# A two-layer hybrid decoder step: w_in columns as filler, an earlier out-norm, an LRU without a reciprocal, part of the SSD on GpSimd

## What is computed

```
h = adaLN1(rms(x));  x += 0.5 * gate1 * (silu(h @ Wg) * (h @ Wu)) @ Wo
u = adaLN2(rms(x)) @ w_in               # [SSD | RG-LRU | HGRN2 | MLA]
y_a = ssd(u_a) * silu(z)                # chunked scan with a state
y_b = lru(u_b) * gelu(gate)
      # r = sigmoid(..), a = exp(-8 r softplus(-lam))
      # bterm = sqrt(-expm1(2 log a)) * (i * xb),  h = a h + bterm
y_c = hgrn2(q, fz, iv) * silu(g)
y_d = attention(prompt), and over 8 cached pages per sample sequence
y   = rms over each 64 features of concat(y_a .. y_d), times out_norm
x  += gate2 * (y @ w_out)
h = adaLN3(rms(x));  x += 0.5 * gate3 * SwiGLU2(h)
```

## Time and profile before

| | |
|---|---|
| Median of 3 runs | 1909.21 us (1907.89 to 1918.09) |
| The profiled execution | 1913.51 us; its span 1911.8 us |
| PE busy / weight loads | 1771.8 us (93%) / 1524.4 us (80%) |
| DVE, ACT, POOL busy | 957.6, 610.9, 237.4 us |
| Mean granted TensorE clock | 0.944 of full speed |
| Chain that ended last | PE 80%, DVE 14%, ACT 3%, DMA 1% |
| Layer 0: w_in's products, mixing, w_out | begin at 311, 466 and 695 us |
| Layer 1: the same | begin at 1249, 1390 and 1614 us |

### The profile page before, as it was taken

How to read it: one execution, slowest core, us unless ns; L and a number is a source line. 1 busy time by engine, 2 the same in 40 slices (tenths; PEclk the granted TensorE clock), 3 DMA queues, 4 the chain that set the end, 5 groups by cost and what they waited for, 6 DMA issues and landing times.

```text
span 1911.8 us, 28829 instructions
## 1 busy us (share of the span) xinstructions
PE 1771.8 (93%) x11864; PEld 1524.4 (80%) x11864; DVE 957.6 (50%) x1729; ACT 610.9 (32%) x972; POOL 237.4 (12%) x434
## 2 busy tenths in 40 slices
PE   4999999999989788999989999999998887899998
PEld 3999996667667556999979999967766664699998
DVE  3544432465775644354445444236767745444443
ACT  2433321033231324343334333111433233333331
POOL 8000003510044000000000000072003210000000
PEclk8999999999887889999999999999998788999999
DMA  9566647862011253554453544493201123435542
GB/s 316 192 198 202 207 144 227 272 213 84 1 53 42 101 186 116 166 182 131 162 172 130 178 135 159 149 255 106 93 25 35 38 67 132 132 133 176 169 145 67
DMA packets 206275, 272.06 MB, mean 142 GB/s; under 512 B 11778, under 2 KB 182238, under 8 KB 206144
## 3 DMA queue, kind: packets, MB, share of 16 engines
q1 hardware_dynamic: 188240, 236.90, 37.9%
q0 software_dynamic: 17904, 33.33, 6.1%
HBM read 264.68 MB, written 5.50 MB: 141 GB/s over the span
## 4 chain that ended last, share of the span: by engine, by line
PE 80%; DVE 14%; ACT 3%; DMA 1%; issue 1%; SPq 0%; DVEq 0%; ACTq 0%
PE bank L782 16%; PE bank L784 16%; PE bank L783 16%; PE bank L913 10%; PE bank L1048 4%; PE bank L1309 4%; PE bank L719 2%; DVE sq L2269 2%; PE bank L1221 1%; PE bank L709 1%; DMA ring<-in_w_ada_dram 1%; DVE big L1995 1%; PE bank L1021 1%; PE bank L1191 1%; DVE zs L1628 1%
## 5 line engine op out<-in xcount | busy, mean ns | idle before, releaser
L784 PE MATMUL bank<-hT_r,ring_r 128*128 128x320 f32 x1408 | 440.5, 313 | 0.0
L784 PEld LDWEIGHTS bank<-hT_r,ring_r 128*128 128x128 f32 x1408 | 267.5, 190 | 0.0
L1636 DVE TENSOR_TENSOR ring_r<-ring,lat_pages_r 128x2048 fp32r<-128x2048 f32 (+1 forms) x68 | 151.4, 2229 | 162.4 <-ACT lat_pages_r L1335 162.4
L782 PE MATMUL bank<-hT_r,lat_pages_r 128*128 128x320 f32 x704 | 218.9, 311 | 13.5 <-DVE gates_r L1668 13.5
L783 PE MATMUL bank<-gates_r,lat_pages_r 128*128 128x320 f32 x704 | 219.3, 312 | 0.0
L784 PE MATMUL bank<-big_r,ring_r 128*128 128x320 f32 x704 | 218.0, 310 | 0.0
L913 PE MATMUL bank<-hT,ring 128*128 128x320 f32 x736 | 209.6, 443 | 4.7 <-DVE hT L1662 4.7
L913 PEld LDWEIGHTS bank<-hT,ring 128*128 128x128 f32 x736 | 140.9, 194 | 65.2 <-issue 11.6
L1335 ACT ACTIVATE lat_pages_r<-ring 128x2048 fp32r<-128x2048 f32 (+1 forms) x68 | 126.4, 1862 | 142.8 <-DMA ring<-in_w_ffn_in_dram 69.4
L782 PEld LDWEIGHTS bank<-hT_r,lat_pages_r 128*128 128x128 f32 x704 | 134.0, 190 | 19.0 <-issue 18.5
L783 PEld LDWEIGHTS bank<-gates_r,lat_pages_r 128*128 128x128 f32 x704 | 133.9, 190 | 0.0
(11 more groups left out here) (536 smaller groups left out, 3252.8 us busy)
## 6 DMA issues: line engine op xcount, KB each, us to landing
ring<-in_w_ffn_in_dram SPq DMA_DIRECT2D x88, 1024.0 KB, 6.1
ring<-in_w_ada_dram SPq DMA_DIRECT2D x60, 1024.0 KB, 6.0
ring<-in_w_ffn_out_dram SPq DMA_DIRECT2D x32, 1024.0 KB, 5.2
ring<-in_w_in_dram SPq DMA_DIRECT2D x22, 1024.0 KB, 7.3
sqk<-in_w_ada_dram POOLq DMA_DIRECT2D x24, 512.0 KB, 7.6
ring<-in_w_ffn_out_dram SPq DMA_DIRECT2D x16, 768.0 KB, 4.4
lat_pages<-in_cache_mla_latent_dram POOLq DMA_DIRECT2D x128, 64.0 KB, 2.2
ring<-in_w_out_dram SPq DMA_DIRECT2D x8, 1024.0 KB, 9.2
```

The costliest lines, as they stand in the source:

```text
L782: mm(out, w_h, x_h, start=start, stop=False)
L784: return mm(out, w_l, x_h, start=False, stop=stop)
L1636: go(v.tensor_tensor(slot_r(n, nk, 256), slot(n, nk, 256), w_hi_r[g % HI][:, 0:nk].bitcast(F32), ALU.subtract), w_low)
```

## The change

- **Filler.** The chunks are reordered: `fz` before `gate` before `q`, `iv`, `g`. The last six chunks (`FILL0 = 19`: `q`, `iv`, `g`, 48 products) are no longer computed by `win`. `fill(n)` issues the next n of their products, all into bank 7, at places in the mixing; `score(b, 4)` puts one behind each of pages 1 to 4 of sequences 0, 1 and 2. `keep_busy` is gone.
- **Order ahead of the SSD.** The transposes of the convolution's last columns, softplus, and the SSD's sums of dt come before the attention's probabilities are turned; DVE computes the SSD's decay before it takes the prompt attention's output, which PE now writes to bank 4.
- **Outputs.** Since `hT` is still read, the mixers' outputs go to a ring slot held for that purpose (`hold`, `mixer_out`): chunks 0, 1 and 4 to 7. Only the LRU's go to `hT`, and only after the last chunk. The list puts an entry without a load at that slot each time its turn comes, until `w_out` is done; the other loads have four slots.
- **Out-norm.** Order of batches: SSD, LRU, attention of the prompt, HGRN2, attention of the samples. ACT takes the root of the sum, with scale and epsilon in the same instruction, in halves; DVE inverts and multiplies in `scale`. PE's products are single, in bank 7. Batches 0 to 2 lie before and between HGRN2's products with the states (L1221).
- **LRU.** (1 + a^2) * tanh(s) in place of 2 lt/(1+lt): ACT adds a square, DVE does one instruction.
- **GpSimd** runs `spread_b` and the states' decay, behind `store_latents` and before the loads of pages for sequences 4 and 5.

```diff
-       (1284, 256), (1540, 256), (1796, 256), (2052, 256), (2308, 256)]
+       (1796, 256), (1284, 256), (1540, 256), (2052, 256), (2308, 256)]
+FILL0 = 19
+HOLD_AT = (11, 11)
-BATCH = [(0, 0, T), (2, 0, T), (4, 0, T), (6, 0, TP), (6, TP, T)]
+BATCH = [(0, 0, T), (2, 0, T), (6, 0, TP), (4, 0, T), (6, TP, T)]
...
+        def skip_held():
+            if held[0] == len(tl) % RING:
+                tl.append((None, 0, 0, *held[1]))
...
+        def mixer_out(l):
+            slot_now = carve(ring, (pos["mixed", l] % RING) * SLOT, 3, 2, T)
+            return [slot_now[:, 0], hT[:, 2:4], slot_now[:, 1], slot_now[:, 2]]
...
+                    pool.wait_ge(ssd_dve, at(ssd_dve, 3))
+                    spread_b(0)
+                    pool.wait_ge(ssd_act, at(ssd_act, 3))
+                    pool.wait_ge(ssd_pe, at(ssd_pe, 4))
+                    for j in range(2):
+                        ends = Es[:, j, P:].rearrange("p (b t) -> p b t", b=NB)[:, :, TS - 1]
+                        pool.tensor_tensor(ssd_state[:, j], ssd_state[:, j], ends.unsqueeze(2).to_broadcast([P, NB, P]),
+                                           ALU.mult).then_inc(decayed, 1)
+                    pool.wait_ge(ssd_pe, at(ssd_pe, 5))
+                    spread_b(1)
                     pool.wait_ge(group_used, at(group_used, 1))
                     load_pages(2)
...
-                        for _ in range(n):
-                            mm(bank[7][:, 0:64], c("ident"), c("ones")[:, 0:64], start=True, stop=True)
+                    def fill(n):
+                        for i, k in itertools.islice(fills, n):
+                            _, _, t, c0 = WCH[i]
+                            if k == 0:
+                                tile_ready(pe, pos["win", l, t])
+                                if i == FILL0:
+                                    pe.wait_ge(att_q, at(att_q, 1))
+                                else:
+                                    pe.wait_ge(*taken(i - 1))
+                            w = slot(pos["win", l, t], 8, WIN[t][1])
+                            ins = mm(bank[7][:, 0:T], w[:, k, c0:c0 + P], hT[:, k], start=k == 0, stop=k == KD - 1)
...
+                    def out_norm(n, half):
+                        if half == 0:
+                            pe.wait_ge(on_sq, at(on_sq, n + 1))
+                        if n or half:
+                            pe.wait_ge(on_root, at(on_root, 2 * n + half))
+                        _, c0, c1 = BATCH[n]
+                        mm(bank[7][:, c0:c1], c("ones64"), norm_tmp(n)[:, half], start=True, stop=True).then_inc(on_pe, 1)
...
-                        o.go(f(lt[:, j], lr[:, j], ACT.Tanh, scale=nlam8[:, j:j + 1]), lru_act)
+                        o.go(f(lt[:, j], lr[:, j], ACT.Tanh, scale=nlam8[:, j:j + 1]))
+                    o.go(f(lm, la, ACT.Square), lru_act)
                     ac.wait_ge(lru_dve, at(lru_dve, 1))
-                    o.go(f(lm, lm, ACT.Sqrt, scale=2.0), lru_act)
+                    o.go(f(lm, lm, ACT.Sqrt), lru_act)
...
-                    do(v.tensor_scalar(lm, lt, 1.0, None, ADD))
-                    do(v.reciprocal(lm, lm))
-                    do(v.tensor_tensor(lm, lm, lt, MUL), lru_dve)
+                    do(v.scalar_tensor_tensor(lm, lm, 1.0, lt, ADD, MUL), lru_dve)
...
+                        ve.wait_ge(on_root, at(on_root, 2 * n + 2))
+                        do(v.reciprocal(x, x))
```

More of the change, by code:

```diff
@@ L984, in _ @@
                     ins.then_inc(mla_pe, 1)
-                    win(20)
+                    pe.wait_ge(conv_done, at(conv_done, 1))
+                    for i in range(FILL0 - 3, FILL0):
+                        pe.wait_ge(*taken(i))
+                    for k in range(KD):
+                        ins = pe.transpose(bank[k // 4][0:27, (k % 4) * P:(k % 4 + 1) * P], last_cols[:, k], c("ident"))
+                    ins.then_inc(turned, 1)
                     pe.wait_ge(mla_dve, at(mla_dve, 7))
@@ L1139, in _ @@
                     new_states(0).then_inc(ssd_pe, 1)
-                    score(1)
+                    fill(4)
+                    turn(1)
+                    fill(4)
+                    score(1, 4)
                     pe.wait_ge(ssd_dve, at(ssd_dve, 6))
@@ L1522, in att_root, with on_square, on_sqrt @@
                         o.go(f(rk[:, b % 2], rk[:, b % 2], ACT.Sqrt), att_rk)
+                    def on_square(n):
+                        ac.wait_ge(mixed, at(mixed, n + 1))
+                        k0, c0, c1 = BATCH[n]
+                        if n == 2:
+                            ac.wait_ge(on_scaled, at(on_scaled, 1))
+                        o.go(f(norm_tmp(n), mixer[k0 // 2][:, :, c0:c1], ACT.Square), on_sq)
+                    def on_sqrt(n):
+                        _, c0, c1 = BATCH[n]
+                        for half in range(2):
+                            ac.wait_ge(on_pe, at(on_pe, 2 * n + half + 1))
+                            o.go(f(norm_tmp(n)[:, half], bank[7][:, c0:c1], ACT.Sqrt, bias=eps, scale=1.0 / 64), on_root)
                     def soft_exp(g):
@@ L2228, in add_from_states @@
                                            bank[bk][:, at_col:at_col + 2 * L].rearrange("p (j n) -> p j n", j=2), ADD))
+                    ve.wait_ge(win_done, at(win_done, len(WCH)))
+                    go(v.tensor_tensor(mixer[1], lh, gelu, MUL))
+                    for n in range(3):
+                        o.tell(mixed)
                     spread_v(0)
                     spread_v(1)
+                    o.settle()
                     go(v.memset(hs[:, :, 0], 0.0))
@@ L2255, in _ @@
                     o.settle()
-                    do(v.tensor_tensor(hT[:, 4:6], oacc, gh, MUL))
-                    for n in range(4):
-                        o.tell(mixed)
+                    do(v.tensor_tensor(mixer[2], oacc, gh, MUL))
+                    o.tell(mixed)
+                    scale(2)
                     att_inv(5)
```

302 lines of the change are left out of this document (147 added, 155 removed), and 4 rows, old and new, of the table WCH.

## The result

| | before | after |
|---|---|---|
| Median of 7 runs | 1913.14 us | 1927.28 us (1924.0 to 1939.09) |
| Ratio, with 95% interval | 1 | 1.0089 (1.0065 to 1.0113) |
| The profiled execution; its span | 1913.51; 1911.8 us | 1924.00; 1922.3 us |
| PE, DVE, ACT, POOL busy | 1771.8, 957.6, 610.9, 237.4 us | 1729.5, 940.0, 620.7, 252.1 us |
| Mean granted clock, profiled | 0.944 | 0.928 |

A forecast was written before the change was run, and what follows sets the result against it. The prediction took PE to bound the FFN and a chain of hand-overs the mixing. A to D gave −38.9 us, E +4 and F +9, together −25.9, so a median of 1883 us, range 1861 to 1902.

The forecast's parts named there:

- A: First chunk to the SSD's transposes: 36.07 us becomes about 25.2, paced by DVE, as chunks move away; −10.9 us a layer.
- B: SSD's transposes to HGRN2: shorter LRU formula, less 0.8 us of page fills left on the path; −3.2 us a layer.
- C: HGRN2's products with the states: out-norm sums and the LRU's product with gelu now stand ahead; +3.0 us a layer.
- D: End of the mixing: ACT's out-norm root no longer waits for DVE's inversion; −8.7 us, layer 1 some 0.7 less.
- The LRU's -4.0: Part of B: the LRU's tanh-to-root steps become an ACT square and one DVE instruction; −4.0 us with its hand-over.
- F: Clock: constants around sequences 4 and 5 go unreplaced; +4.5 us a layer, +9 in all, ends −5 and +20.
- E: Weight ring with one slot held: FFN tile 1 and two layer 0 tail tiles land late; +4 us in all.
- Rival 2: Fills lie on the path in the mixing: a third of their 26 us shows, +17.6, giving 1901 us; chance 0.15.
- rival 4: Clock falls through the whole mixing, 0.83 to 0.60 giving 1926 us; slower from about 0.64 down; chance 0.05.
- Rival 3: GpSimd is dear (5.3 us and more) or slows DVE: +3 to 6 us a layer, 1892 us; chance 0.10.

The follow-up runs named there:

- z_all: Changed kernel with x_tail's order, x_busy's constants, y_sp's early softplus and z_order's order around the SSD's new states; 1898.1 us, 0.9940 to before.
- z_order: x_tail with the order of the kernel before around the SSD's new states, on both DVE and PE; 1916.3 us, 1.0030 to before.
- x_empty: Changed kernel with only one 64-column constant per filler chunk, the last six chunks not computed; 1915.7 us, 1.0029 to before.
- x_tail: Changed kernel with the out-norm's prompt-attention and HGRN2 batches moved out of the third softmax's way; 1912.9 us, 1.0007 to before.
- z_all2: z_all run once more, unchanged; 1897.6 us on one chip, 0.9935 to before.
- x_const: Changed kernel with its 48 filler products per layer replaced by 64-column constants, the last six chunks not computed; 1916.9 us, 1.0017 to before.
- y_pool: x_tail with GpSimd's two spreads and two decays back on DVE; 1926.6 us, 1.0088 to before.
- z_none: Kernel before without any of its 152 constants in a layer; 1923.4 us, 1.0071 to before.
- x_busy: Changed kernel with constants put back in the second half of the mixing; 1920.1 us, 1.0035 to before.
- v_more: z_all with 42 more constants in a layer, in the second half; 1907.2 us, 0.9980 to before.
- y_sp: x_tail with softplus and the instructions that feed it moved earlier, into DVE's wait for chunks; 1910.3 us, 0.9993 to before.

## Why the prediction was wrong

Against the forecast, the four sections are short by 39 us in the profiled executions: A by 11, B by 18, C by 3, D by 8. The transposes stood at 469.8 us where 465 was forecast, w_out at 699.6 where 675 was.

- **A, right in size but not reached.** The step failed at "with PE thinned out DVE paces" and its 25.2 us, which came to 28.7 in layer 0: softplus and the copies of the last columns, which chunks had covered, were counted as DVE's work and not as PE's wait of 5.01 us, with half the clock behind it. That the sixth chunk's time would just cover the wait for the rotary queries was 0.9 and 2.4 us too good. z_all has A at -10.0 and -9.3.
- **B, wrong, and the largest miss of a section.** "Most of that hides ... I leave 0.8 on the path": layer 0 and 1 lost 7.6 and 10.3 us against the forecast. The clock is not the reason, with 0.90 and 0.86 where 0.86 and 0.88 had been; PE's idle time grew by 6.2 and 4.7 us. The forecast had no term for the new order around the SSD's states, in which PE waits for DVE's scores and turned states. z_all, with the old order there, has B at 75.8 and 75.7 at a clock of 0.90, so a part is that order; z_order had next to nothing of it by itself. The LRU's -4.0 is right (-5.8 and -3.4 alone). How much is the filler's isn't taken apart: x_empty, with next to no filler, still has B at 77.0 and 77.5, but at a clock of 0.77 and 0.78. And 12 of the 48 fills stand in A, where the forecast counted them; what it set against 39.3 us of constants as 26 us of products was 19 us.
- **C, +3.0, with F's +4.3 behind it: right in the sum** (8.7 and 8.6 against 7.3), and that is partly luck. The records of L1298 took 2.7 us more, not 4.3, and the four sums before their end some 4.4 us, not 2.2, most of them at half clock too.
- **D, -8.7: the mechanism was right, its cover wrong.** "ACT is never behind DVE" came true for the out-norm's root. What was missed is who then waits for ACT: the softmax's exponential, 5.6 us. x_tail has -8.5 and -7.7.
- **E, +4: the sum is near, its parts are not.** The two waits for ada tiles in layer 0 take 3.4 us, where 2 were forecast; from w_out's start to FFN's it is 50.4 us against 50.9, where 1 us more was forecast for each layer.
- **F, mis-sized.** It was priced from two stretches, +9 us for both layers with an end of +20. The mean clock fell by 0.016 in the profiled execution and by 0.025 over all seven, not by the 0.012 that the forecast's 0.78 in the mixing would have made, and by the slope 0.025 costs some 28 us. The price per 0.01 was nearly right (11.5 us for 0.1 of 229 us is 9.6 for 0.01 of the whole, where 11.3 is measured). In the mixing the clock came as forecast (0.79). But it also fell where it had been 0.99 to 1.00, at the end of the projection, where PE is idle for lack of the very chunks that were taken out; the forecast had the front at full clock.
- The path without the clock: -35 forecast (A to E), about -11 had by the changed kernel, about -22 by z_all2, by the column at 0.948. So of the 46 us between the forecast and the mean of the seven some 24 are the path's and 19 the clock's. This division is an estimate.
- **Rivals.** Rival 2 (a third of the filler shows, +17.6) came for the most part in the changed kernel: 12 to 14 us by x_const and x_empty, 20 to 26 at equal clock. Of rival 4 (the clock) the outcome happened, slower than before, but not the mechanism: the mean in the mixing was 0.79, where I had put its point at 0.64. It needed no collapse, since A, B and D fell short at the same time. Rival 3 didn't happen; GpSimd took 1.9 to 2.1 us, under the 2.5 assumed. By the Trainium skill ("GPSIMD Engine Reference", "Performance versus the Vector engine") I had estimated 2.25 us; the trace agrees to within a sixth. Its rule to keep elementwise work on the Vector engine is true of the instruction (1.9 against 1.2 us) and wrong for this kernel: y_pool, which follows it, is 14 us slower.
- The Trainium skill's "Loop structure matters more than you think" ("TensorE: Matmul & The Clock Gate"), that waits between bursts bring the clock down, I had called agreed in part and given 0.05 for its full extent. z_none agrees with it: without constants, 0.83 becomes 0.78 in the mixing.

**A version faster than both** is z_all: 0.6% under the kernel before (z_all2, the same kernel again, 0.65%), 1.5% under the changed one. It is the change, with the out-norm's order of x_tail, constants in the second half, softplus early, and the old order around the new states.

## What to carry to other kernels

Taking work off TensorE has two prices: who waits for what the work covered, and what the clock then does to everything else. Read the clock in each stage, the one with the work removed included, and get the price of 0.01 from repeated executions of one kernel. When steps are moved ahead of a chain, follow each engine's queue to the instruction just behind them: the out-norm's roots held back by 5.6 us an exponential that all engines needed. Check each section's clock before the clock is blamed: it was lower in A, C and D, and hardly in B, which lost most. And before a part is judged useless, undo it in the best version, not in the first: the filler here looked worthless in the changed kernel, where leaving its products out gave 12 to 14 us and section A had won 11 by moving them, and was a gain of 15 to 22 in the repaired one.

## Not expected of the hardware

- One and the same kernel gets another mean clock in each execution (0.942 to 0.955 for the one before), and its time goes with it (correlation -0.83 over 90 executions). A profile is one draw: the changed kernel's profiled execution, at 0.928, was the fastest of its seven.
- In the products of 8 columns the clock fell to 0.50 while PE was busy all the time, whatever stood ahead of them: in the changed kernel the first 128 records took 5.74 us and the next 128 7.00; with 14 constants ahead (x_busy) it was 5.14 and 7.00, with 22 (v_more) 3.90 and 6.94.
- Behind PE's wait of 5 us in the projection the sums took 2.05 us, at a granted clock of 0.50; with the wait at 0.61 us (y_sp, layer 1) they took 1.13. For how long the clock then stays low differs: the same stretch to the transposes in layer 1 had 0.67 in x_tail and 0.87 in z_order, after the same wait.
- Constants help only to a point: none is 12 us slower in the kernel before, and 42 more per layer in z_all are 9 slower.
